# Two blocks on one core: the norms between them by token tile, the experts' overflow inside the experts' block

## The reference

```
h = h + hierarchical_moe(v, ...)          # two expert rows per token, each times its gate
x = rms_norm(h, norm_final)               # the row that block two adds to at its end
hn = rms_norm_2(x, norm_w)                # read by every product with w_in
u = (hn @ w_in)[..., 2560:3584]           # input of the state space part; gates, q, k, v are other columns
```

## Time and profile before

| | us |
|---|---|
| median of 3 runs | 4087.4 (4086.02 to 4092.1) |
| profiled execution, whole | 4089.98 |
| profiled execution, span | 4088.2 |
| PE busy | 3671.9 (90%) |
| DVE busy | 1002.5 (25%) |
| ACT busy | 536.1 (13%) |
| POOL busy | 236.2 (6%) |

### The profile page before, as it was taken

The page is one execution under the profiler, slowest core; times in us unless marked ns, Lnnn a source line. Parts: engine busy times, 40 slices in busy tenths (PEclk is TensorE's granted clock), DMA queues, the critical chain, the costliest instruction groups (busy, mean ns, idle before and its releaser), DMA issues. The chain is left out here.

```text
span 4088.2 us, 44543 instructions
## 1 busy us (share of the span) xinstructions
PE 3671.9 (90%) x19165; PEld 1897.7 (46%) x19165; DVE 1002.5 (25%) x1879; ACT 536.1 (13%) x928; POOL 236.2 (6%) x238
## 2 busy tenths in 40 slices
PE   4999999999799887777777719999999999999999
PEld 2455555555445432232222218554444444555588
DVE  2234545457411200000000044137000120222100
ACT  1122221212202100000000010100110110421000
POOL 0000000000000000000000000011200000111000
PEclk9999999999899899999999959999999999999999
DMA  3222111211141799999999863225343212223331
GB/s 90 62 55 52 44 44 44 64 44 63 63 157 39 319 421 421 422 422 422 421 420 417 345 183 112 83 78 129 93 97 103 98 62 82 71 71 136 103 103 62
DMA packets 324524, 666.07 MB, mean 163 GB/s; under 512 B 42685, under 2 KB 245863, under 8 KB 269958
## 3 DMA queue, kind: packets, MB, share of 16 engines
q1 hardware_dynamic: 316021, 632.16, 42.8%
q0 software_dynamic: 8336, 31.47, 2.1%
HBM read 636.44 MB, written 43.91 MB: 166 GB/s over the span
## 5 line engine op out<-in xcount | busy, mean ns | idle before, releaser
L2120 PE MATMUL stream_bank<-whole_big 128*128 128x512 f32 x1920 | 830.2, 593 | 0.0
L1769 PE MATMUL experts_run_bank<-whole_big 128*64 128x512 f32 x2048 | 489.8, 625 | 172.9 <-DMA whole_big<-in_expert_w_gate 102.5
L357 PE MATMUL first_bank<-whole_big 128*128 128x512 f32 x1344 | 636.9, 611 | 9.1 <-DMA whole_big<-in_w_in 9.1
L2120 PEld LDWEIGHTS stream_bank<-whole_big 128*128 128x128 f32 x1920 | 363.2, 190 | 450.7 <-issue 450.2
L1769 PEld LDWEIGHTS experts_run_bank<-whole_big 128*64 128x64 f32 x2048 | 168.9, 143 | 493.2 <-issue 493.1
L357 PEld LDWEIGHTS first_bank<-whole_big 128*128 128x128 f32 x1344 | 241.5, 191 | 271.6 <-issue 251.6
L2118 PE MATMUL stream_bank<-whole_big 128*128 128x256 f32 x1536 | 334.1, 380 | 5.4 <-DMA whole_big<-in_w_in 3.9
L2111 PE MATMUL stream_bank<-whole_big 128*128 128x512 f32 x768 | 336.8, 594 | 0.9 <-DVE whole_big L2823 0.5
L2118 PEld LDWEIGHTS stream_bank<-whole_big 128*128 128x128 f32 x1536 | 292.7, 191 | 46.6 <-DMA whole_big<-in_w_in 4.3
L1789 PE MATMUL experts_run_bank<-whole_big 128*64 128x512 f32 x1024 | 230.0, 596 | 35.2 <-DMA whole_big<-in_expert_w_down 22.6
L1828 DVE TENSOR_TENSOR whole_big<-whole_big,experts_run_bank 128x512 f32<-128x512 f32 x16 | 11.0, 688 | 907.2 <-PE experts_run_bank L1769 907.2
(11 more groups left out here) (414 smaller groups left out, 2707.3 us busy)
## 6 DMA issues: line engine op xcount, KB each, us to landing
whole_big<-in_expert_w_gate SPq DMA_DIRECT2D x128, 1024.0 KB, 28.0
whole_big<-in_expert_w_up SPq DMA_DIRECT2D x128, 1024.0 KB, 29.3
whole_big<-in_expert_w_down SPq DMA_DIRECT2D x128, 1024.0 KB, 26.7
whole_big<-in_w_in SPq DMA_DIRECT2D x110, 1024.0 KB, 7.7
whole_big<-in_w_out SPq DMA_DIRECT2D x32, 1024.0 KB, 7.4
gates_two<-whole_big SPq DMA_DIRECT2D x40, 256.0 KB, 7.9
whole_big<-gates_two POOLq DMA_DIRECT2D x40, 256.0 KB, 3.0
whole_big<-in_x SPq DMA_DIRECT2D x2, 4096.0 KB, 15.3
```

The source lines that it names most:

```text
L357: mm = pe.matmul(bank[:, :], slot[:, k, sub * P:(sub + 1) * P], u_T[:, k, :], start=(k == 0), stop=(k == KD - 1))
L1769: mm = pe.matmul(bank[self.half(h), :], self.x_T[:, PARTS * q + k, self.half(h)], self.ring[slot][:, k, :], start=(q == 0 and k == 0), sto ...
L2120: mm = pe.matmul(bank[:, :], slot[:, k, (u % 2) * P:(u % 2 + 1) * P], left[:, k, :], start=(k == 0), stop=(k == KD - 1))
```

## The change

The overflow loop, formerly a block, stands at the end of each engine's list in `experts`, behind a test of the count that each engine reads at the start. DVE takes two of the four evacuations of y from ACT. Semaphores of stream one are cleared ahead of the experts' block; those of the pairs (kept scope) after it. The ring of block two moves to the end of the arena, over three of the experts' last slots, and SP asks for panels 0 and 1, the gain row and the results of tiles 0 and 1 from within the experts' block. `finish_block_one` and the norm of block two are gone as blocks: class `Finish` does both norms of one token tile inside `stream_two`. DVE adds the gated rows in halves, multiplies by norm_final, and forms both roots from two sums. PE multiplies each 128x128 piece of the row by a diagonal matrix that holds the reciprocal of the row's second root, which turns and scales in one product; DVE and ACT evacuate two banks each with the gain of the second norm. ACT then scales the row in place for x2. The first 8 units of u go by token tile, two panels for each tile; the tables come behind unit 7; `turn_u` goes behind units 10, 12, 15 and 17. The inputs of the state space part are loaded in two parts, with the results of tile 2 behind the first and those of tile 3 behind the second.

```diff
+    def put_y(self, eng, n, place, quarters, first=False):
         if not first:
-            act.wait_ge(self.scattered, 16 * n)
-        for q in range(4):
+            eng.wait_ge(self.scattered, 16 * n)
+        for q in quarters:
             if q < 3:
-                act.wait_ge(self.y_mm, 3 * n + q + 1)
+                eng.wait_ge(self.y_mm, 3 * n + q + 1)
             else:
-                self.done(act, place, 2)
-            act.activation(self.y[0:self.n, q * T:(q + 1) * T], self.y_bank[q][0:self.n, :], ACT.Copy).then_inc(self.y_ready, 1)
+                self.done(eng, place, 2)
+            to, bank = self.y[0:self.n, q * T:(q + 1) * T], self.y_bank[q][0:self.n, :]
+            if quarters[0]:
+                eng.tensor_copy(to, bank).then_inc(self.y_ready, 1)
+            else:
+                eng.activation(to, bank, ACT.Copy).then_inc(self.y_ready, 1)
...
+    def load_results(self, sp, results, t):
+        view = results.rearrange("(t p c) d -> p t c d", p=P, c=2)
+        for half in range(2):
+            cut = slice(half * D // 2, (half + 1) * D // 2)
+            sp.dma_start(self.results[t % 2][:, :, cut], view[:, t, :, cut]).then_inc(self.result_in[t % 2][half], 16)
...
+                count = number(sp)
                 with sp.Fori(0, turns - 1) as i:
                     for c in range(RING, 2 * x.chunks + RING):
                         load(i, c)
                 for c in range(RING, 2 * x.chunks):
                     load(turns - 1, c)
+                with sp.If(count > 0):
+                    with sp.Fori(0, count) as b:
+                        e = sp.value_load(over_expert[0:1, bass.ds(b, 1)], min_val=0, max_val=E - 1)
+                        sp.wait_ge(free, b + 1)
+                        for chunk in range(o.chunks):
+                            o.load(sp, e, chunk, chunk, None)
+                    sp.wait_ge(done, 1)
+                for slot in (3, 2, 1):
+                    sp.wait_ge(x.used[slot], 2 * 3 * turns)
+                    if slot == 2:
+                        dense.load(sp, 0)
+                        dense.load(sp, 1)
+                sp.dma_start(entry.gain_row, a["norm_final"].unsqueeze(0).broadcast_to([P, D])).then_inc(entry.gain_in, 16)
+                sp.wait_ge(done, 1)
+                for t in range(2):
+                    entry.load_results(sp, results, t)
...
                 turn(turns - 1, True)
                 pool.wait_ge(x.scattered, 16 * PAIRS)
+                with pool.If(count > 0):
+                    o.last_row, o.last_result = x.last_row, x.last_result
...
+                        pool.wait_ge(o.scattered, 16 * b + 16)
+                        pool.sem_inc(free, 1)
+                pool.sem_inc(done, 1)
...
             @block.scalar
             def _(act):
+                count = number(act)
                 act.sem_inc(x.y_ready, 4)
+                act.sem_inc(o.y_ready, 4)
                 for b in range(2):
-                    x.activate(act, b, place(0, b), first=(b == 0))
+                    x.activate(act, b, place(0, b))
+                    x.put_y(act, b, place(0, b), (0, 1), first=(b == 0))
                 with act.Fori(1, turns) as i:
                     for b in range(2):
                         x.activate(act, 2 * i + b, place(i, b))
+                        x.put_y(act, 2 * i + b, place(i, b), (0, 1))
+                with act.If(count > 0):
+                    with act.Fori(0, count) as b:
...
+    def sync(self, sp, results, t):
+        sp.wait_ge(self.sem["added"], 4 * (t - 2) + 4)
+        self.entry.load_results(sp, results, t)
+
+    def store(self, sp, x2, t):
+        sp.wait_ge(self.sem["scaled"], t + 1)
+        sp.dma_start(x2[t * P:(t + 1) * P, :], self.rows[:, t, :]).then_inc(self.sem["stored"], 16)
+
+    def vector(self, dve, t):
+        sem, entry = self.sem, self.entry
+        if self.steps is None:
+            self.steps = Steps(dve, sem["step"])
+
+        def do(instruction):
+            self.steps.did(instruction)
+            self.steps.wait()
+
+        for half in range(2):
+            dve.wait_ge(entry.result_in[t % 2][half], 16 * (t // 2 + 1))
+            row, cut = self.half(t, half), slice(half * D // 2, (half + 1) * D // 2)
+            for c in range(2):
+                if c:
+                    dve.wait_ge(sem["added"], 4 * t + 2 * half + 1)
+                dve.scalar_tensor_tensor(out=row, in0=entry.results[t % 2][:, c, cut], scalar=self.gates[:, t, c:c + 1], in1=row,
+                                         op0=ALU.mult, op1=ALU.add).then_inc(sem["added"], 1)
+        if t == 0:
+            dve.wait_ge(entry.gain_in, 16)
+        for half in range(2):
+            row, cut = self.half(t, half), slice(half * D // 2, (half + 1) * D // 2)
+            dve.wait_ge(sem["added"], 4 * t + 2 * half + 2)
+            dve.wait_ge(sem["squared"], 4 * t + half + 1)
+            dve.tensor_tensor(row, row, entry.gain_row[:, cut], ALU.mult).then_inc(sem["gained"], 1)
+        dve.wait_ge(sem["squared"], 4 * t + 4)
+        first, second, both = self.sums[:, t, 0:1], self.second[:, t:t + 1], self.both[:, t, :]
+        do(dve.tensor_reduce(self.sums[:, t, :], self.stat[:, t, :, :], AX.X, ALU.add))
+        do(dve.tensor_scalar(first, first, 1.0 / D, 1e-6, ALU.mult, ALU.add))
+        do(dve.reciprocal(both[:, 1:2], first))
+        do(dve.tensor_tensor(second, self.sums[:, t, 1:2], both[:, 1:2], ALU.mult))
+        do(dve.tensor_scalar(second, second, 1.0 / D, 1e-6, ALU.mult, ALU.add))
+        dve.tensor_tensor(both[:, 0:1], first, second, ALU.mult).then_inc(sem["varied"], 1)
+        dve.wait_ge(sem["rooted"], t + 1)
+        do(dve.reciprocal(self.inv[:, t:t + 1], self.root[:, t, 0:1]))
+        dve.tensor_scalar(self.diag[:, t, :], self.ident[:, :], self.inv[:, t:t + 1], None, ALU.mult).then_inc(sem["diag_ready"], 1)
+        for b in range(2):
+            dve.wait_ge(sem["turned"], 4 * t + b + 1)
+            dve.tensor_tensor(self.h_T[:, 4 * b:4 * b + 4, t * P:(t + 1) * P], self.bank[b][:, :].rearrange("p (k s) -> p k s", s=P),
+                              self.gain[:, 4 * b:4 * b + 4].unsqueeze(2).broadcast_to([P, 4, P]), ALU.mult).then_inc(sem["ready_v"], 1)
+
+    def scalar(self, act, t):
+        sem = self.sem
+        for kind in range(2):
+            for half in range(2):
+                n = 4 * t + 2 * kind + half
+                if kind:
+                    act.wait_ge(sem["gained"], 2 * t + half + 1)
+                else:
+                    act.wait_ge(sem["added"], 4 * t + 2 * half + 2)
+                if n:
+                    act.wait_ge(sem["squared"], n)
+                act.activation(self.junk, self.half(t, half), ACT.Square, accum_out=self.stat[:, t, kind, half:half + 1]).then_inc(sem["squared"], 1)
+        act.wait_ge(sem["varied"], t + 1)
+        act.activation(self.root[:, t, :], self.both[:, t, :], ACT.Sqrt).then_inc(sem["rooted"], 1)
+        for b in range(2, 4):
+            act.wait_ge(sem["turned"], 4 * t + b + 1)
+            for j in range(4):
+                k = 4 * b + j
+                act.activation(self.h_T[:, k, t * P:(t + 1) * P], self.bank[b][:, j * P:(j + 1) * P], ACT.Identity,
+                               scale=self.gain[:, k:k + 1]).then_inc(sem["ready_a"], 1)
+        act.wait_ge(sem["rooted"], t + 1)
+        act.activation(self.rows[:, t, :], self.rows[:, t, :], ACT.Identity, scale=self.root[:, t, 1:2]).then_inc(sem["scaled"], 1)
+
+    def tensor(self, pe, t):
+        sem = self.sem
+        pe.wait_ge(sem["diag_ready"], t + 1)
+        for b in range(4):
+            for j in range(4):
+                at = (4 * b + j) * P
+                mm = pe.matmul(self.bank[b][:, j * P:(j + 1) * P], self.rows[:, t, at:at + P], self.diag[:, t, :], start=True, stop=True)
+            mm.then_inc(sem["turned"], 1)
+        pe.wait_ge(sem["ready_v"], 2 * t + 2)
+        pe.wait_ge(sem["ready_a"], 8 * t + 8)
```

```diff
-STARTS = list(range(0, 16, 4)) + list(range(16, 76, 2)) + list(range(76, 156, 4))
+STARTS = [0, 1, 8, 12] + list(range(16, 76, 2)) + list(range(76, 156, 4))
...
+    return unit % 2 if unit < 8 else max(i for i in range(PANELS) if STARTS[i] <= unit)
...
-    return (STARTS + [156])[panel + 1] - 1
+    return 6 + panel if panel < 2 else (STARTS + [156])[panel + 1] - 1
+
+
+def token_of(unit):
+
+    return unit // 2 if unit < 8 else unit % 4
...
+RING2_AT = RING_AT + XW
+GAIN_AT, DIAG_AT, JUNK_AT = 24000, 26048, 26560
...
+        U_TURN_AFTER = {10: 0, 12: 1, 15: 2}
...
             def _(sp):
+                def store_u(u):
+                    dense.freed(sp, u)
+                    t, panel = token_of(u), panel_of(u)
+                    sp.dma_start(u_dram[t * P:(t + 1) * P, panel * PW:(panel + 1) * PW], u_stage[:, u % 4, :]).then_inc(stored[u % 4], 16)
+
                 def take_u(p):
                     for i in range(4):
-                        sp.wait_ge(stored[i], 16 * (p + 1))
```

(56 more changed lines are left out.)

254 lines of the change are left out of this document (102 added, 152 removed).

## The result

The changed kernel took 4050.7 us (median of four executions, 4048.3 to 4055.6), beside 4089.2 for the kernel before on the same chip: a ratio of 0.991 with a 95% interval of 0.989 to 0.9925. Predicted were 4051 and a gain of 36.0; measured are 38.5 between the medians and 34.4 between the spans of the two profiled executions, 4088.2 and 4053.8. The profiled one is the slowest of the four (4055.56), and that will matter: part of the time in this stage is not the same in each execution.

A forecast was written before the change was run, and what follows sets the result against it. Experts bound by transfers, then PE from w_in's load on, with a 104.2 us hole between. Unit 8 at 2469.7 instead of 2510.59, less 0.9, gains 40.0; less 4.0 at entry, 36.0: 4087.4 to 4051, range 4040 to 4066.

The forecast's parts named there:

- Entry, +4.0: Experts' entry: semaphore clearing, barrier and count read delay a transfer-bound stage; cost 4.0, taken between 2.5 and 7.
- Early loads: End of experts: w_in loaded early removes a 7.74 wait, but the last scatter lands in 7, between 4.5 and 9.1.
- Front as a whole: Last scatter to DVE's first adds: landing 2357.3, results asked for 2358.3, there 2363.5, adds from 2364.
- No drain behind the table load: ACT before tile 0's Sqrt: the skill's drain of about 1.38 per table load left out, following the trace.
- Tile 0, 21.7: PE in block two: diagonal products 5.35, ACT's last pieces 1.5, units 0 and 1 13.8, clock lapse 1.
- Tiles 1 to 3, 23.2 each: PE, per tile: products 3.5, ACT's pieces 1.5, row scaling and copy 2.4, two units 13.8, clock lapse 2.0.
- Tables and panel 2, 3.1: PE between units 7 and 8: tables 2.6, and 0.5 for panel 2 of w_in, just hidden.
- the 30 I named: DVE's table work, ending before PE's transpose needs it: 30 or more left to spare.
- No result was late: Rival: results of tile 2 or 3, queued on SP behind C or B, ten late at one: 4061, chance 0.13.
- The front lost 3: Rival: nothing gained at the front, adds from 2372 as before, entry costs 7: 8 + 3 lost, 4062, chance 0.10.
- PE did not stay at 1.2 GHz: Slower rival: waits of 3.9 keep PE at 1.2 GHz through the whole stage, costing 63: 4114, chance 0.05.
- Three pairs without a lapse: Rival: no clock lapse between tiles, plus short ends of entry and landing, 7 + 2: 4042, chance 0.12.

The follow-up runs named there:

- The repeat: The changed kernel run once more, unedited, as the yardstick for the other runs: 4052.1 us, ratio 0.991 to the kernel before.

## Why the prediction was right

The mechanism was the one predicted: the serial tail between experts and block two became a chain for one tile, the rest of it went beside PE's products, and the span is 34.4 shorter, for 36.0 predicted. Unit 8 was due at 2473.7 with the entry's 4 and came at 2475.29. The 1.6 between is the sum of larger errors of both signs, so that the number is this close is in part luck:

- **Entry, +4.0: wrong, it cost 0.** The wait grew by 2.1, under my lower bound of 2.5, and the clock gave it back. I had priced the wait alone and not the products behind it, which are what SP waits for; that they ran at 1.2 GHz could be read in the trace of before, in a stretch I did not open. The run with two more barriers shows the other side: a delay paid, and no clock to pay it back.
- **Early loads: right that the scatter pays for them, 2.5 too little.** I took 7 between 4.5 and 9.1; it was 9.5. It took 9.4 to 10.3 with four loads of w_in under way, and 4.5 to 5.0 with two or none. That is what the rule gave that I had weighed and then split the difference with (the Trainium skill, DMA: Bandwidth & Descriptors, "Queues, rings and completion order"); the trace agrees: while the scatter was under way in the changed kernel the DMA engines were busy with w_in and the gain row (share 1.18 in 2352 to 2354), and with two loads early they had little else to do by then (0.17 in the same stretch of the kernel with panel 1 in the next block).
- **Front as a whole: 4.6 late without the entry's 4.** The adds were due at 2364 and start at 2368.57: 1.5 are older than the entry, 2.5 the scatter, 1.3 the results' transfer (7.0 for the 5.7 between my two dates; before, twice the bytes took 7.66), less 0.7 since the request came 0.3 behind the landing and not 1.0. The results' transfer I had scaled by its bytes at 421 GB/s, but in the three windows from 2362 to 2368 the DMA moved 104, 215 and 289 GB/s, and 422 only from 2368 on. In the kernel with panel 1 in the next block, where no load stands ahead of it, it took 7.2, so the early loads aren't the reason. From the adds to the first diagonal products it is 11.0 for 11.3. So they stand at 2379.59 where I said 2379: the unpaid entry and the late front cancel.
- **No drain behind the table load: right.** Sqrt starts at 2378.82, where the load ends (2377.53 and 1.28). The 1.38 of drain (the Trainium skill, ScalarE: Activation LUTs, "What ACT_TABLE_LOAD costs") isn't in this row either.
- **Tile 0, 21.7: it took 20.8.** The lapse of 1 that I charged didn't come.
- **Tiles 1 to 3, 23.2 each: 24.2, 24.1 and 24.1, 2.8 more in all.** The gap was 3.63 for 3.9, the products 3.7 for 3.5, two units without a lapse 13.9 for 13.8, the lapse 2.7 to 3.0 for 2.0. The repeat had 1.4, 1.7 and 0: the size varies, and what I took lies inside.
- **Tables and panel 2, 3.1: 2.5.** No wait for panel 2. DVE's tables have 29.7 to spare for the 30 I named: the second make_ba ends (L2867) at 2531.8, and its transposes on PE (L2464) start at 2561.51. That is luck too. Counted from unit 8's start I had DVE's end at 45 and PE's date at 78; they are 56.5 and 86.2. By the sum of the prediction's own rows, a start at 2470 and the 63.7 from 2446 to 2509.7, the end would have been 64 behind unit 8 and only 14 to spare; DVE came sooner mainly because it idles 7.0 for ACT in its tables and idled 14.1 before.
- **The rivals.** No result was late: after tile 0 DVE idles for none. The front lost 3 beside what it inherited, not 8. PE did not stay at 1.2 GHz. Three pairs without a lapse were in no profiled execution of the changed kernel; with the shorter gap they were in each. This rival's price was wrong: the short ends of entry and landing are 1.5 and 2.5, 4 together and not 2, so it stood for 4040.

One judgement was missing rather than wrong. The 3.9 and the lapse stood in my sum as the cost of norms by tile. They are the cost of where ACT scales the row, and with units by panel they would not have been there; I put no price on the order that the change replaced.

Still open is why the clock falls behind one gap of 3.6 and not behind the next, and what holds the results' transfer at 100 to 300 GB/s for its first microseconds. The norms by tile as a whole and the overflow inside the experts' block were not undone in any run either: what they gained is read from the two traces.

## What to carry to other kernels

When a sum says that an engine waits a few microseconds for a copy, look at what stands ahead of that copy in the other engine's list before you accept the wait: here 2.2 less of waiting, three times, and the lapses that went with it were worth 11. Price a load that is moved forward three times: for who shares the DMA engines with it, for the engine that has to issue it behind other loads, and for the block that can't close until it has. And a total that comes out right says little of its terms: 4.0 charged for something that cost nothing hid 3 at the front and 1.4 in block one.

## What the hardware showed that I had not expected

- The same gap of 3.6 on PE in the same place is followed by a lapse to 1.2 GHz that costs 3.0, 1.5 or nothing, from one execution to the next and within one; behind gaps of 1.3 to 1.7 none was seen in this stage. A delay can also come with a gain of nearly its length: with 3.53 of wait ahead of 16 transposes the products behind them started at 2.4 GHz, with 1.42 and with 4.84 at 1.2.
- SP's issue isn't free. Four loads of w_in, 1 MB each, took it 7.9 with nothing else under way, 18.9 when asked for behind the experts' weights and 15.1 behind the results; two took 12.5 behind the weights, 8.5 and 6.9 behind the results. A load of 1 MB of the experts' weights took 1.4 (11.12 for 8), so it isn't the bytes alone. What sets the time was not tried.
- One indirect scatter took 4.5 to 5.0 with at most two loads of w_in asked for ahead of it and 9.4 to 10.3 with four (4 MB), which go by another queue.
